# The sample's decode attention and tail moved between the expert gathers of the prompt

## The reference

```
[q | k | v | u] = x @ w_in + b_in
att = mixture of dilated causal windows (128,1), (512,4), (2048,16), 8 heads of 64, ALiBi
ssm = S5: h[t] = a * h[t-1] + z * (B u[t]) complex, y = Re(C h) + D u
z = gelu(ssm); ssm_out = z * sigmoid(z @ w_glu + b_glu)
h = LN1(ALPHA * x + concat(rms(att), rms(ssm_out)) @ w_out + b_out)
q = h @ w_pq; top 16 of each of two key sets; top 16 of the 256 sums: 16 experts, 8 heads
ffn = sum over the 128 (expert, head) of softmax * gelu(h . peer_u[e]) * peer_v[e]
y = LN2(ALPHA * h + ffn + sigmoid(h @ w_ple_gate) * (p @ w_ple))
```

## Time and profile before

| | |
|---|---|
| median of the runs | 2153.49 us |
| profiled execution | 2152.67 us |
| its span | 2150.9 us |
| busy: PE, DVE, ACT, POOL | 1540.3, 1346.7, 671.1, 745.8 us |
| bytes by DMA | 702.57 MB, of them 604.02 MB gathers |
| chain that ended last | PE 35%, DMA 29%, DVE 19% |

### The profile page before, as it was taken

The page is one execution under the profiler, slowest core; times in us unless marked ns, Lnnn a source line. Parts: engine busy times, 40 slices in busy tenths (PEclk is TensorE's granted clock), DMA queues, the critical chain, the costliest instruction groups (busy, mean ns, idle before and its releaser), DMA issues.

```text
span 2150.9 us, 22852 instructions
## 1 busy us (share of the span) xinstructions
PE 1540.3 (72%) x7052; PEld 782.2 (36%) x7052; DVE 1346.7 (63%) x3180; ACT 671.1 (31%) x2436; POOL 745.8 (35%) x784
## 2 busy tenths in 40 slices
PE   8988899999866676666766776557666656676654
PEld 6577775465333343223333423112221222121111
DVE  3339971236688888878888867664554555444544
ACT  0012232220234444434444423233332333232322
POOL 0001115200244444334444434354342444443442
PEclk9988889999988778797877788677888788778887
DMA  7010017872599999999999999999999999999996
GB/s 298 1 53 1 1 50 304 352 288 121 176 409 411 398 399 412 376 373 406 409 414 393 406 341 404 413 393 376 419 407 366 379 422 411 418 388 355 419 422 281
DMA packets 102550, 702.57 MB, mean 327 GB/s; under 512 B 12080, under 2 KB 16816, under 8 KB 25392
## 3 DMA queue, kind: packets, MB, share of 16 engines
q0 software_dynamic: 82944, 604.02, 69.9%
q1 hardware_dynamic: 16816, 89.94, 10.9%
q10 hardware_dynamic: 2688, 7.34, 1.2%
HBM read 686.95 MB, written 4.87 MB: 322 GB/s over the span
## 4 chain that ended last, share of the span: by engine, by line
PE 35%; DMA 29%; DVE 19%; issue 8%; ACT 4%; POOL 4%; POOLq 0%; ACTq 0%; DVEq 0%; SPq 0%
DMA R<-d_uv,E 29%; PE bank L895 9%; DVE R L1632 7%; PE bank L588 4%; PE bank L700 4%; POOL R L549 4%; PE bank L803 3%; PE bank L840 3%; PE bank L859 2%; PE bank L582 2%; PE bank L637 1%; PE bank L652 1%; DVE E L1571 1%; DVE E L1568 1%; ACT E L1187 1%
## 5 line engine op out<-in xcount | busy, mean ns | idle before, releaser
L895 PE MATMUL bank<-R,E 128*32 128x512 f32 x2304 | 758.6, 813 | 549.6 <-ACT E L1192 542.9
L549 POOL DMA_INDIRECT R<-d_uv,E x576 | 676.2, 1174 | 1055.9 <-PE bank L895 505.5
L1632 DVE CUSTOM_DVE_ANT_0 R<-R,E 128x1024 f32<-128x1024 f32 x576 | 693.4, 1224 | 456.1 <-DMA R<-d_uv,E 434.8
L895 PEld LDWEIGHTS bank<-R,E 128*32 128x32 f32 x2304 | 239.1, 134 | 1019.4 <-ACT E L1192 742.1
L1184 ACT ACTIVATE E<-E 128x2 f32<-128x2 f32 x288 | 57.8, 201 | 369.5 <-DVE E L1632 362.5
L1192 ACT ACTIVATE E<-fold,E 128x32 f32<-128x32 f32 x576 | 153.5, 313 | 9.6
L859 PEld LDWEIGHTS bank<-E,W 128*128 128x128 f32 x1280 | 144.4, 192 | 19.9 <-issue 18.6
L1137 ACT CAST E<-E 128x4 uint32<-128x4 f32 (+1 forms) x146 | 27.8, 191 | 389.9 <-DVE E L1632 387.4
L859 PE MATMUL bank<-E,W 128*128 128x128 f32 (+1 forms) x1280 | 148.0, 276 | 1.1 <-ACT E L1097 1.1
L1187 ACT ACTIVATE E<-E 128x1 f32<-128x1 f32 x576 | 138.2, 287 | 12.7
L588 PE MATMUL bank<-E,W 128*128 128x288 f32 x384 | 96.2, 414 | 8.4 <-DMA E<-d_xT 8.4
(11 more groups left out here) (277 smaller groups left out, 1643.3 us busy)
## 6 DMA issues: line engine op xcount, KB each, us to landing
R<-d_kc SPq DMA_DIRECT2D x8, 2560.0 KB, 12.7
R<-d_vc SPq DMA_DIRECT2D x8, 2560.0 KB, 10.0
R<-d_uv,E POOLq DMA_INDIRECT x576
W<-d_w_pq SPq DMA_DIRECT2D x4, 2048.0 KB, 15.9
E<-E ACTq DMA_DIRECT2D x56, 128.0 KB
W<-d_w_in SPq DMA_DIRECT2D x3, 2048.0 KB, 15.4
R<-d_w_out SPq DMA_DIRECT2D x2, 2048.0 KB, 8.0
W<-d_w_gate SPq DMA_DIRECT2D x2, 2048.0 KB, 14.8
```

The source lines that it names most:

```text
L549: pool.indirect_dma_start(ring[r], None, A["uv"], bass.IndirectOffsetOnAxis(ap=stage[:, half, s:s + 1], axis=0),).then_inc(landed[r], 16)
L895: last = mm(acc[p0:p0 + TG, half * 512:half * 512 + 512], wsel[:, r, :], ring[r][:, D + half * 512:D + half * 512 + 512], start=False, sto ...
L1632: last = nc.vector.tensor_tensor_reduce(ring[r][:, 0:D], ring[r][:, 0:D], hrep[:, js[s], :], 1.0, 0.0, ALU.mult, ALU.add, dots[:, x, s:s + 1])
```

## The change

The decode attention of the sample leaves the place ahead of the gathers. After the prompt's attention, the GLU, the output projection and the first picks are done for the four prompt blocks alone, and the gathers start when these are done. The sample's q, k, v and u are copied aside by GpSimd. The list of `order_of_work` is now made from a table that says what stands ahead of each half-turn: from half-turn 57 on the decode attention, in eleven steps per sequence, a new sequence every four half-turns; from 91 the sample's GLU, sums, projection and LN1; from 102 its picks; from 118 the gates and `finish`, in the order 2, 0, 1, 3, 4, every four half-turns. The cache tiles have one buffer each, in W, where w_pq lay, and SP loads w_out, w_glu, the three rows and w_pq a second time for the sample. In `ssm_out` and `s_ssm_out` the loop over the four products stands outside that over the four column groups.

```diff
-OUT_BANK = [0, 4, 4, 0, 4]
...
+OUT_BANK = [0, 4, 4, 0, 0]
+BLOCK_TURNS = 2 * EXP // RING
+DECODE_AT = 57
+DECODE_TURNS = 4
+SAMPLE_AT = DECODE_AT + DECODE_TURNS * (NB - 1) + 7
+TURN_AT = SAMPLE_AT + 10
+PICK_AT = TURN_AT + 3
+GATE_AT = PICK_AT + 13
+GATE_TURNS = 4
+FINISHED = [2, 0, 1, 3, 4]
...
+    def pick(n, t, coming):
+        if n >= 2 and n != 4 * QB:
+            at[t + 1].append(("lay", *picks[n - 1]))
...
+        at[t + 4].append(("resolve", *picks[n]))
+    for n in range(1, 4 * QB):
+        pick(n, 4 * (n - 1), [x for x in picks[n + 1:n + 2] if x[0] < QB])
+    at[4 * (4 * QB - 1) + 1].append(("lay", *picks[4 * QB - 1]))
+    at[BLOCK_TURNS + 1].append(("put_by", 0))
+    at[2 * BLOCK_TURNS].append(("put_by", 1))
+    at[DECODE_AT - 1].append(("s_set",))
+    for b in range(NB):
+        t = DECODE_AT + DECODE_TURNS * b
+        for k, what in ((0, "s_scores"), (1, "s_scores_rest"), (2, "s_bias"), (3, "s_exp"), (4, "s_norm"),
+                        (5, "s_turn"), (6, "s_copy"), (7, "s_values"), (8, "s_copy_out"), (9, "s_turn_out"),
+                        (10, "s_out")):
+            at[t + k].append((what, b))
+    t = SAMPLE_AT
...
+    at[t + 9].append(("s_normal",))
+    n = 4 * QB
+    at[TURN_AT].append(("turn", QB))
+    at[TURN_AT + 1].append(("ask", *picks[n]))
+    at[TURN_AT + 2] += [("ask_out", *picks[n]), ("match", *picks[n])]
+    at[TURN_AT + 3].append(("match_out", *picks[n]))
+    for c in range(4):
+        pick(n + c, PICK_AT + 4 * c, picks[n + c + 1:n + c + 2])
+    at[PICK_AT + 17].append(("lay", *picks[-1]))
+    for k, b in enumerate(FINISHED):
+        t = GATE_AT + GATE_TURNS * k
+        at[t].append(("gate_turn", b))
+        at[t + 1].append(("gate", b, 0))
+        at[t + 2] += [("gate_out", b, 0), ("gate", b, 1)]
+        at[t + 3].append(("gate_out", b, 1))
+        if b < QB:
+            at[t + 5].append(("finish", b))
...
+    for n in range(total + 1):
+        if at[n] or n % BLOCK_TURNS in (0, 2, 30, 31) or n == total:
+            if n > turn:
+                order.append(("experts", turn, n))
+            turn = n
+            order += at[n]
+    return order + [("finish", QB)]
...
             sp.wait_ge(sc_biased, len(UNITS))
-            for n, (kind, b) in enumerate(CACHE_TURNS):
-                if n == 1:
-                    sp.wait_ge(y_used, 4 * QB)
-                    sp.wait_ge(carried, 4 * QB)
-                if n >= 3:
-                    what, b0 = CACHE_TURNS[n - 3]
-                    sp.wait_ge(ss_full if what == "k" else so_full, b0 + 1)
-                if kind == "k":
-                    load(kcS[n % 3], A["kc"][b][:, :, 0:NK], in_cache[n % 3])
-                else:
-                    load(vcS[n % 3], A["vc"][b][:, 0:KT, :], in_cache[n % 3])
-                if n == 5:
-                    sp.wait_ge(sbu_full, 2)
-                    load(glu, A["glu"], in_glu)
-            sp.wait_ge(ss_full, NB)
             load(wout[0], A["w_out"][0].rearrange("p (c n) -> p c n", c=DC), in_out[0])
-            sp.wait_ge(so_full, NB - 1)
+            sp.wait_ge(hs_ready, 4 * QB + 1)
             load(wout[1], A["w_out"][1].rearrange("p (c n) -> p c n", c=DC), in_out[1])
-            sp.wait_ge(glu_full, CT)
-            load(W[:, 3, :], A["w_pq"][0], in_pq[0])
+            load(rows1, A["rows1"], in_rows1)
             sp.wait_ge(kv_left, 16 * (BLOCKS + 1))
-            sp.wait_ge(qblk_set, 1)
-            sp.wait_ge(sy_used, 1)
+            sp.wait_ge(q_kept, 1)
+            sp.wait_ge(k_kept, 1)
+            sp.wait_ge(u_kept, 1)
+            sp.wait_ge(v_kept, 1)
+            sp.wait_ge(y_used, 4 * QB)
             for b in range(BLOCKS):
                 t0, n = tokens_of(b)
                 load(hS[0:n, b, :], A["x_rows"][t0:t0 + n, :], in_xr)
             load(keysT, A["keysT"], in_keys)
-            sp.wait_ge(so_full, NB)
-            load(rows1, A["rows1"], in_rows1)
+            sp.wait_ge(sbu_full, 2)
+            load(W[:, 3, :], A["w_pq"][0], in_pq[0])
+            sp.wait_ge(mixed, CT)
             load(W[:, 0, :], A["w_pq"][1], in_pq[1])
-            sp.wait_ge(so_turned, NB)
+            sp.wait_ge(sq_full, 1)
             load(W[:, 1, :], A["w_pq"][2], in_pq[2])
-            sp.wait_ge(sq_full, 1)
-            load(W[:, 2, :], A["w_pq"][3], in_pq[3])
-            sp.wait_ge(out_full, BLOCKS)
+            sp.wait_ge(out_full, QB)
             sp.wait_ge(h_ready, 1)
             for j in range(SG):
                 for s in range(SG):
                     load(hrep[TG * s:TG * s + TG, j, :], hS[TG * j:TG * j + TG, 0, :], in_hrep[j // 2])
+            sp.wait_ge(sy_full, 1)
+            load(W[:, 2, :], A["w_pq"][3], in_pq[3])
             sp.wait_ge(carried, 4 * QB)
             sp.dma_start(A["stp_out"], sm[:, 14:16, :]).then_inc(outs, 16)
+            sp.wait_ge(sx_ready, 1)
             for c in range(2):
                 sp.dma_start(A["sts_out"][:, c], xs_last[c]).then_inc(outs, 16)
-            sp.wait_ge(pq_full, 4 * BLOCKS)
+            def keys(b):
+                if b >= 1:
+                    sp.wait_ge(ss_full, b)
+                load(kcS, A["kc"][b][:, :, 0:NK], in_kc)
+            def values(b):
+                if b >= 1:
+                    sp.wait_ge(so_full, b)
+                load(vcS, A["vc"][b][:, 0:KT, :], in_vc)
+            sp.wait_ge(pq_full, 4 * QB)
+            keys(0)
+            load(sbias[0:ST], A["sbias"], in_sb)
+            values(0)
+            for b in range(1, NB):
+                keys(b)
+                if b >= 2:
+                    values(b - 1)
+            sp.wait_ge(ss_full, NB)
+            load(s_wout[0], A["w_out"][0].rearrange("p (c n) -> p c n", c=DC), in_out[0])
+            values(NB - 1)
+            sp.wait_ge(sp_turned, NB)
+            load(s_glu_w, A["glu"], in_glu)
+            sp.wait_ge(so_full, NB)
+            load(s_wout[1], A["w_out"][1].rearrange("p (c n) -> p c n", c=DC), in_out[1])
+            load(s_rows1, A["rows1"], in_rows1)
+            sp.wait_ge(so_turned, NB)
+            sp.wait_ge(sq_full, 2)
+            load(W[:, 3, :], A["w_pq"][0], in_pq[0])
+            sp.wait_ge(out_full, BLOCKS)
+            load(W[:, 0, :], A["w_pq"][1], in_pq[1])
+            load(W[:, 1, :], A["w_pq"][2], in_pq[2])
+            sp.wait_ge(h_ready, BLOCKS)
+            load(W[:, 2, :], A["w_pq"][3], in_pq[3])
+            sp.wait_ge(pq_full, 4 * QB + 2)
...
-            pool.wait_ge(out_full, BLOCKS)
+            pool.wait_ge(out_full, QB)
...
-                for j in range(4):
-                    t = 4 * q + j
-                    for x, c in enumerate((Csc[:, t, 0, :], Cneg[:, t, :], Csc[:, t, 1, :], Csc[:, t, 1, :])):
+                for x in range(4):
+                    for j in range(4):
+                        t = 4 * q + j
...
             def s_scores(b):
-                n = k_turn(b)
-                keys = kcS[n % 3]
-                pe.wait_ge(in_cache[n % 3], 16 * (n // 3 + 1))
-                if b >= 1:
+                pe.wait_ge(in_kc, 16 * (b + 1))
+                if b == 0:
+                    pe.wait_ge(qblk_set, 1)
+                    pe.wait_ge(s_ready, 4 * QB)
+                else:
                     pe.wait_ge(ss_biased, b)
-                for n0 in range(0, NK, 512):
-                    n1 = min(n0 + 512, NK)
-                    for c in range(CT):
-                        last = mm(bankf[0:ST, n0:n1], qblk[:, b, c, :], keys[:, c, n0:n1],
-                                  start=(c == 0), stop=(c == CT - 1))
-                    if n1 == FIRST_BANKS:
-                        last.then_inc(ss_first, 1)
+                s_keys(b, 0, 512)
+                s_keys(b, 512, FIRST_BANKS).then_inc(ss_first, 1)
+            def s_scores_rest(b):
+                s_keys(b, FIRST_BANKS, NK)
                 for c in range(CT):
-                    last = mm(bankf[0:ST, NK:SK], qblk[:, b, c, :], kT[:, c, SEQ:TOK],
+                    last = mm(bankf[0:ST, NK:SK], qblk[:, b, c, :], kS[:, c, :],
                               start=(c == 0), stop=(c == CT - 1))
                 last.then_inc(ss_full, 1)
...
-            pe.wait_ge(qblk_set, 1)
             pe.wait_ge(sc_biased, len(UNITS))
             pe.wait_ge(pt_ready, len(UNITS))
-            s_scores(0)
             s_ssm_in(0)
+            pe.wait_ge(in_glu, 16)
+            pe.wait_ge(z_ready, 1)
+            for c in range(2):
+                glu_tile(c)
             s_ssm_in(1)
-            for b in range(NB):
-                s_turn(b)
-                if b >= 1:
-                    s_turn_out(b - 1)
-                if b + 1 < NB:
-                    s_scores(b + 1)
-                if b == SSM_OUT_AT:
-                    s_ssm_out()
-                if b in GLU_BEFORE:
-                    glu_tile(GLU_BEFORE[b])
-                s_values(b)
-                if b in GLU_AFTER:
-                    glu_tile(GLU_AFTER[b])
-            s_turn_out(NB - 1)
+            for c in range(2, CT):
```

(19 more changed lines are left out.)

518 lines of the change are left out of this document (281 added, 237 removed).

## The result

The changed kernel takes **2163.6 us** (median of 20 runs, 2154.9 to 2180.7) against 2153.6 for the kernel before (20 runs): the ratio is 1.0048, 95% interval 1.0033 to 1.0062. The change makes the kernel slower by half a per cent. The forecast was 2150 us, with faster as the likeliest side; the time lies inside the range of 2130 to 2174 and on the other side of no change.

What follows compares the result with a forecast made beforehand. Bytes were taken to bind the gather stage, and PE the decode stage. The first gather 150 us earlier, 144 us of bytes and 3 us of new steps gave -3 us on a 2150.9 us span, so 2150 us, range 2130 to 2174.

Steps and rivals of the forecast that it cites:

- part 1: Prompt's stage: the new matmul order in `ssm_out` and moved `qblk` zeroing end it 13 us earlier, bounds 3 and 22.
- part 2: From the prompt's end to `project(0)`: 30 us instead of 153, bounds 27 and 36, so `project(0)` starts 136 us earlier.
- The stages and the bound: Four stages; the gather stage is bound by bytes, DMA busy to 0.99; the decode stage stands on PE's account.
- Rival E: `ssm_out`: the new order frees nothing, accumulating matmuls still go one after the other; the 13 become 1, 2162 us; chance 0.10.
- Part 3: From `project(0)` to the first gather: 14 us less than 86, by no longer waiting for the sample's third of the projections.
- Part 4: Gather stage: 59.7 MB moved there or loaded twice, at 415 GB/s, add 144 us, bounds 140 and 151.
- part 5: New steps between half-turns: decode steps cost nothing, the two sample projections and closer gates 3 us together.
- C: PE's queue between half-turns: long steps free ring slots late, up to +40 us, 2187, or a third, 2163; chance 0.15.
- D: Gather stage: mixed traffic runs slower, 341 GB/s, so 59.7 MB take 175 us, +28, 2181 us; chance 0.08.
- B: Head wins more: all 22 us of `ssm_out` count, bytes run at 427 GB/s, no gap; -19, 2134 us; chance 0.25.

Runs made afterwards that it cites:

- the kernel with the later chain: The changed kernel with GpSimd's chain of sample states started only behind the fourth GLU product: 2153.1 us, ratio 1.0000 against the kernel before.

## Why the prediction was wrong, step by step

The kernel came out 10 us slower where 3 us faster was forecast. Two steps of the prediction failed, both ahead of the gathers: the 9 us taken for DVE's waits in part 1, and the 2.5 us for the steps between the last GLU tile and the sums in part 2. What follows counts in the profiles.

**The stages and the bound: right.** Bytes bind the gather stage (share 0.99, 398 GB/s).

**Part 1, 13 us: wrong, about 4.** The step that failed is "Of these I take 9", of the 12.5 us that DVE waits for PE's scores. DVE's waits for PE's scores fell only from 12.5 us in nine places to 9.1 in five. What `ssm_out` freed on PE became waiting for ACT's exponentials, which in turn wait for DVE (24.7 us ahead of L663 from 160 to 316 us, 13.5 before), and at the lower granted clock the other products ran longer. The lower bound of 3 was near the right value. With the order exchanged alone, in either kernel, the time doesn't move (ratios 1.0049 against 1.0048, and 1.0002, each to about 0.0025, 5 us): 13 us are ruled out. Rival E, with the forecast's 13 turned into 1, named the right size for a wrong reason: the records do run at 0.03 us each.

**Part 2, 30 us: wrong, 43.** Its own terms were right where PE ran at 2.4 GHz: product 3.7, tile pair 7.1. Three were mis-sized. The DVE steps before the sums were priced at 2.5 us and the wait was 9.8: that was GpSimd's chain beside them, whose start near 326 us the prediction had worked out (338.2 measured) and checked only against the first gather (36 us to spare, 41 measured). The sums took 7.0 and not 3.6, at a granted clock of 0.50 behind the pause. And the first product and the GLU tiles took 5.4 us more, mostly at the lower clock, where 1.5 had been allowed for it, and 1 for a table load that the slow product hid. 30 + 7.3 + 3.4 + 5.4 - 2.5 = 43.6, against 42.9 measured. With the chain moved away, the same stretch took 29.6 us.

**Part 3, 14 us: right,** 15.8 (70.2 us from `project(0)` to the first gather against 86.0). Together the first gather is at 430.9 and not at 411: 8.8 us by part 1 (the stage's end at 317.8 and not 309), 12.9 by part 2, and 1.8 back. The prediction had named the mark: wrong if the first gather comes after 430 us, "because of the GLU row, GpSimd's chain or a load" that comes late. It came at 430.9, and both the GLU row and the chain had a part, the chain not by its own end, as meant there, but by what it did to DVE.

**Part 4, 144 us: right.** 15.25 MB more in all, 717.82 MB; the stage grew by 147.1 us with part 5. By the kernels with fewer bytes, a MB costs about 2.1 us (81 us for 37.7, 23 for 11.0) where 422 GB/s would make it 2.4. That would leave some us more to part 5 than 3, but the difference is within what these runs scatter, and the remainder was not measured by itself.

**Part 5, 3 us: right in sum.** The decode steps cost nothing at four half-turns, though the scores step, put at 5.9 us and so under the gate's 7.0, takes 7.1 at the high clock. Where the forecast put the 3 us, the sample's tail and the gates, the rate is 387 GB/s over 589 us; spreading the gates did not bring it back.

**The rivals.** C was refuted for four half-turns; at three its loss appears, by a wait for the keys. D was refuted: plain loads beside gathers move 422 GB/s. The rule of the Trainium skill named there (DMA: Bandwidth & Descriptors, Where 436 GB/s comes from), about 358 GB/s between HBM and SBUF, is contradicted by these 422 over 350 us. B failed with part 1. The measured time lies nearest to what was written of E and of a light C, but neither mechanism was at work; the true one, contention of GpSimd with DVE, was not among the rivals.

So the sum was -130 + 147 - 1 = +16 on the span of one execution, and +10 in the medians. With the chain out of DVE's way it is 0: the kernel with the later chain has the ratio 1.0000 (0.9977 to 1.0022).

**What stays open:** whether the lower activity alone lowers the clock in the prompt's stage, which no run isolates; what decides between the two clock levels at 317 us, which differ from kernel to kernel with the same code up to there, and perhaps from run to run; and why gates five half-turns apart are slower than four. The 20 runs of the changed kernel lie within 26 us and the 20 beside them of the kernel before within 11, but 30 further runs of the kernel before lie within 24, so that is no difference between the kernels.

## What to carry to other kernels

When work is taken out of a stretch, ask what will now run beside the work that is left. A chain on GpSimd that did no harm in its old place made DVE's operations with two SBUF inputs two to four times as long in its new one (0.69 to 1.37 and 2.72 us), and one wait puts it back beside work that doesn't mind. Time saved on an engine that isn't the bound should be priced at its lower bound. And a stage that bytes bind is paid per MB, about 2.1 us here. In the forecast itself the head won 150 us, the bytes that only moved took 107 of them, and the 15 MB loaded twice took 37 of the 43 that were left, before any detail went wrong.

## What the runs showed of the hardware that was not expected

- DVE operations with two SBUF inputs of 128 x 512 took 1.37 to 2.72 us beside GpSimd operations of 1.9 to 2.7 us, and 0.69 without; one with a single such input and a scalar per row took 1.25 and 2.12 and 0.48 without; those that read PSUM kept their time (1.28 and 1.22 us). GpSimd pays too: four of its operations of 0.5 us took 0.9 to 1.5 beside DVE's residual steps (382.6 to 387.9 us).
- 56 copies of 128 KB within SBUF by DMA cost the gather stage 37 us in one kernel and 30 in the other, for 7.34 MB that at 422 GB/s would be 17; ACT did them for less, at some 16 us of its own time per block.
- 32 matmul records of 128 columns over four column groups took 1.0 us at the high clock, and 2.4 in the old order, and the program took the same time.
- Behind a pause of 2.6 us, PE's next 16 column sums (32 records) took 4.8 us, 7.0 behind one of 9.8 us, and 3.6 with the pause filled.
- Three half-turns for a sequence's key tile with one buffer left PE waiting for the load up to 10.0 us and GpSimd for slots up to 18.8.
